# The 16 meta tokens' matmuls split over four column groups of TensorE

## What is computed

```python
def even_layer(x, ...):
    h = rms_norm(x, norm_g)
    proj = h @ w_in                               # 528 x 1024 @ 1024 x 3072
    q, k, v, gate_b, gate_c, u = jnp.split(proj, cuts, axis=-1)
    att = stick_breaking_attention(q, k, v)       # 8 heads of 64
    conv = gate_b * causal_short_conv(gate_c * u, conv_w)
    return jnp.concatenate([att, conv], axis=-1) @ w_out

def peer_ffn(x, ...):
    q = (hb @ w_query).reshape(t, 8, 2, 128)
    s = jnp.einsum('thpc,phkc->thpk', q, keys)
    sv, si = lax.top_k(s, 16)                     # then top 16 of the 16 x 16 sums
    u = expert_u[idx]
    act = gelu(einsum('tnd,td->tn', u, hb))
    return einsum('tn,tnd->td', gate * act, expert_v[idx])

for layer in range(2):
    h = h + even_layer(h) if layer == 0 else h + odd_layer(h)
    h = h + peer_ffn(h)
return h[:, 16:]
```

## Time and profile before

| | us |
|---|---|
| median of 3 runs | 3180.07 (3178.79 to 3183.22) |
| the profiled execution | 3176.12 |
| its span on the core | 3174.4 |
| PE busy | 2720.4 (86%) |
| DVE busy | 2100.6 (66%) |
| POOL busy | 997.9 (31%) |
| ACT busy | 596.8 (19%) |

### The profile page before, as it was taken

One profiled execution on the slowest core, in us unless ns is written; L12 is line 12 of the kernel. 1 busy time (PEld: TensorE's weight loads), 2 busy tenths in 40 slices (PEclk: granted clock), 3 DMA queues, 4 the chain that ended last, 5 costly groups with the idle time before them and its releaser, 6 DMA issues.

```text
span 3174.4 us, 29633 instructions
## 1 busy us (share of the span) xinstructions
PE 2720.4 (86%) x6788; PEld 1244.4 (39%) x6788; DVE 2100.6 (66%) x6388; ACT 596.8 (19%) x1775; POOL 997.9 (31%) x1106
## 2 busy tenths in 40 slices
PE   7999998898798879868898888878898898887777
PEld 3575343343343334324343333433344343333333
DVE  1123158888678767857688758875787678755554
ACT  1026211211111111112111221112112211111111
POOL 0000004333333333323333333333333333333332
PEclk9999999999999999989999999999999999889999
DMA  3121129999999999999999999999999999999998
GB/s 107 53 93 60 52 106 375 415 384 391 417 421 420 406 407 421 421 411 406 413 421 409 405 399 417 415 392 403 416 403 393 421 419 414 393 420 422 421 406 333
DMA packets 166368, 1135.00 MB, mean 358 GB/s; under 512 B 21136, under 2 KB 22160, under 8 KB 30768
## 3 DMA queue, kind: packets, MB, share of 16 engines
q0 software_dynamic: 149760, 1090.59, 84.0%
q1 hardware_dynamic: 16432, 42.62, 3.6%
HBM read 1130.97 MB, written 2.10 MB: 357 GB/s over the span
## 4 chain that ended last, share of the span: by engine, by line
DMA 43%; PE 39%; DVE 9%; issue 7%; ACT 1%; SPq 0%; POOLq 0%; DVEq 0%; ACTq 0%; POOL 0%
PE psum L1377 19%; DMA ring_early<-in_peer_uv,idx_u 12%; DMA ring_early<-in_peer_vu,idx_u 12%; DMA ring_late<-in_peer_uv,idx_u 10%; DMA ring_late<-in_peer_vu,idx_u 8%; PE psum L986 6%; PE psum L565 3%; PE psum L659 3%; DVE ring_early L1471 3%; PE psum L691 2%; PE psum L596 2%; DVE ring_late L1471 1%; DVE work L1112 1%; DVE si L1110 1%; PE psum L1018 1%
## 5 line engine op out<-in xcount | busy, mean ns | idle before, releaser
L1377 PE MATMUL psum<-ring_early,w_col 128*128 128x512 f32 x2864 | 1384.2, 627 | 234.2 <-ACT w_col L1424 203.7
L1471 DVE SCALAR_TENSOR_TENSOR ring_early<-ring_early,psum 128x1024 f32<-128x1024 f32 x716 | 871.2, 1217 | 440.8 <-DMA ring_early<-in_peer_vu,idx_u 225.7
L1377 PEld LDWEIGHTS psum<-ring_early,w_col 128*128 128x128 f32 x2864 | 565.7, 202 | 972.5 <-issue 732.7
L1377 PE MATMUL psum<-ring_late,w_col 128*128 128x512 f32 x1296 | 639.9, 633 | 124.0 <-ACT w_col L1424 94.1
L1358 POOL DMA_INDIRECT ring_early<-in_peer_vu,idx_u x360 | 339.2, 942 | 685.1 <-DVE ring_early L1471 300.5
L1358 POOL DMA_INDIRECT ring_early<-in_peer_uv,idx_u x356 | 337.2, 947 | 619.6 <-DVE ring_early L1471 302.0
L1471 DVE SCALAR_TENSOR_TENSOR ring_late<-ring_late,psum 128x1024 f32<-128x1024 f32 x324 | 394.6, 1218 | 204.6 <-DMA ring_late<-in_peer_uv,idx_u 133.6
L1424 ACT ACTIVATE w_col<-ident,weight 128x128 f32<-128x128 f32 x1024 | 343.4, 392 | 675.6 <-DVE weight L1453 660.0
L1377 PEld LDWEIGHTS psum<-ring_late,w_col 128*128 128x128 f32 x1296 | 256.6, 202 | 453.4 <-issue 325.4
L1418 ACT ACTIVATE ge<-ga 128x4 f32<-128x4 f32 x260 | 53.3, 205 | 1354.4 <-DVE ga L1439 1354.4
L986 PE MATMUL psum<-wq,hbT 128*128 128x512 f32 x512 | 276.7, 628 | 19.9 <-DVE work L1112 18.8
(11 more groups left out here) (220 smaller groups left out, 1785.1 us busy)
## 6 DMA issues: line engine op xcount, KB each, us to landing
wq<-in_peer_w_query SPq DMA_DIRECT2D x16, 1024.0 KB, 18.0
w_ring<-in_even_w_in SPq DMA_DIRECT2D x6, 2048.0 KB, 8.0
ring_early<-in_peer_vu,idx_u POOLq DMA_INDIRECT x360, 12.0
ring_early<-in_peer_uv,idx_u POOLq DMA_INDIRECT x356, 11.8
w_ring<-in_even_w_out SPq DMA_DIRECT2D x1, 4096.0 KB, 13.8
ring_late<-in_peer_vu,idx_u POOLq DMA_INDIRECT x162, 12.4
ring_late<-in_peer_uv,idx_u POOLq DMA_INDIRECT x162, 12.4
hres<-in_x SPq DMA_DIRECT2D x4, 512.0 KB, 4.9
```

What stands on the lines that cost most here:

```text
L1377: ins = nc.tensor.matmul(y_ps[:, half, :], w_col[:, i % W_SLOTS, :], v_cell(at)[:, 512 * half:512 * half + 512], start=False, stop=i == CH ...
L1471: nc.vector.scalar_tensor_tensor(out=cell, in0=cell, scalar=1.0, in1=rows, op0=ALU.mult, op1=ALU.mult, accum_out=dot[par][:, i:i + 1]).the ...
```

## The change

- Query, key and value of the meta tile: the 512 moving columns are cut in four of 128, each of which is multiplied into its own 32 partitions of the bank (partition 32c), for each k all four in turn. ACT brings them together with four copies of 16x128 instead of one of 16x512.
- The out-projection of the meta rows: 1024 columns in four of 256, in the same way, in one bank instead of two. PE adds the meta rows of `hres` through four identity matmuls, and ACT copies back with four copies of 16x256 where DVE added two halves. Projections are now counted from tile 0 (`i - 1`), and the waits on `s_proj` and `s_mix` are shifted by two to match.
- The meta queries: the four groups of `wq` go into four column groups, k outermost, with 32 stationary columns (16 tokens and 16 columns of zeros, cleared once by POOL). ACT then copies one 128x512 instead of four 16x512, PE transposes four 128x128 pieces instead of sixteen 16x128 ones, and ACT copies 128x512 again.
- The scores: still 16 matmuls of 128 columns, over the four column groups, into one bank.
- Top-k of the meta tokens reads that bank. The four spreading copies and the clearing of `cand` go. PE doesn't wait for them any longer before it transposes tile 0; before projection 4 it waits until top-k has read the bank (`s_read` 1).

```diff
@@ mixer_tensor
                     n = rows_of(t)
+                    if t == XT:
+                        for k in range(KD):
+                            for c in range(4):
+                                last = nc.tensor.matmul(psum[32 * c:32 * c + META, 4 + i % 4, 0:P], hT[:, k, cols_of(t)],
+                                                        w_ring[:, g % 2, k, P * c:P * c + P],
+                                                        start=(k == 0), stop=(k == KD - 1))
+                                if k == KD - 1 and c < 3:
+                                    last.then_inc(s_qkv_m, 1)
+                        last.then_inc(s_qkv_ps, 1)
+                        continue
...
             pe.wait_ge(s_qkv, 3 * TILES)
+            pe.wait_ge(s_qkv_mc, 9)
...
-            project_tensor(pe, 0)
-            project_tensor(pe, 1)
+            for c in range(4):
+                nc.tensor.matmul(psum[32 * c:32 * c + META, 0, 0:256], ident[0:META, 0:META], META_ROWS[:, 256 * c:256 * c + 256],
+                                 start=True, stop=False)
+            for k in range(KD):
+                for c in range(4):
+                    last = nc.tensor.matmul(psum[32 * c:32 * c + META, 0, 0:256], catT[:, k, cols_of(XT)],
+                                            w_out_sb[:, k, 256 * c:256 * c + 256], start=False, stop=(k == KD - 1))
+                    if k == KD - 1:
+                        last.then_inc(s_mproj, 1)
@@ project_tensor
-                pe.wait_ge(s_mix, max(i - 1, 4))
+                pe.wait_ge(s_mix, max(i - 3, 2))
+                pe.wait_ge(s_read, 1)
@@ mixer_scalar
+                    if t == XT:
+                        act.wait_ge(s_qkv_m, 3 * g + 3)
+                        for c in range(4):
+                            nc.scalar.copy(qkv[0:n, t, g, P * c:P * c + P], psum[32 * c:32 * c + META, 4 + i % 4, 0:P]
+                                           ).then_inc(s_qkv_mc if c < 3 else s_qkv, 1)
+                        continue
@@ start_tensor
-            if isinstance(job, int) and job == 1:
-                pe.wait_ge(s_spread, GROUPS)
-            elif isinstance(job, int) and job == 2:
+            if isinstance(job, int) and job == 2:
@@ meta_queries_tensor
-            for g in range(GROUPS):
-                for k in range(KD):
-                    last = nc.tensor.matmul(META_BANKS[g][0:META, :], hbT[:, k, 0:META], wq[:, k, 512 * g:512 * g + 512],
+            for k in range(KD):
+                for g in range(GROUPS):
+                    last = nc.tensor.matmul(FA[32 * g:32 * g + 32, :], hbT[:, k, 0:32], wq[:, k, 512 * g:512 * g + 512],
                                             start=(k == 0), stop=(k == KD - 1))
-                last.then_inc(s_meta_q_ps, 1)
-            for g in range(GROUPS):
-                pe.wait_ge(s_meta_q, g + 1)
-                for i in range(LISTS):
-                    at = META * (LISTS * g + i)
-                    last = nc.tensor.transpose(QUERY_BANK[:, at:at + META], META_Q[g][:, P * i:P * i + P], ident[0:META, 0:META])
+                    if k == KD - 1:
+                        last.then_inc(s_meta_q_ps, 1)
+            pe.wait_ge(s_meta_q, 1)
+            for i in range(LISTS):
+                last = nc.tensor.transpose(FB[:, P * i:P * i + P], q_sb[:, P * i:P * i + P], ident[:, :])
@@ meta_scores_tensor
-            for i in range(LISTS * GROUPS):
-                at = P * (i % LISTS)
-                last = nc.tensor.matmul(META_BANKS[i // LISTS][0:META, at:at + P], metaT[:, META * i:META * i + META],
-                                        keysT[:, i, :], start=True, stop=True)
+            for i in range(LISTS):
+                for g in range(GROUPS):
+                    last = nc.tensor.matmul(LATE_BANK[32 * g:32 * g + 32, P * i:P * i + P], q_T[:, i, 32 * g:32 * g + 32],
+                                            keysT[:, LISTS * g + i, :], start=True, stop=True)
+                    if i == LISTS - 1 and g < GROUPS - 1:
+                        last.then_inc(s_spread, 1)
@@ meta_scalar
-            for g in range(GROUPS):
-                act.wait_ge(s_meta_q_ps, g + 1)
-                nc.scalar.copy(META_Q[g], META_BANKS[g][0:META, :]).then_inc(s_meta_q, 1)
+            act.wait_ge(s_meta_q_ps, GROUPS)
+            nc.scalar.copy(q_sb[:, :], FA).then_inc(s_meta_q, 1)
             act.wait_ge(s_q_ps, 1)
-            nc.scalar.copy(metaT, QUERY_BANK[:, 0:LISTS * GROUPS * META]).then_inc(s_qT, 1)
-            act.wait_ge(s_cleared, 1)
-            act.wait_ge(s_sc, 1)
-            for g in range(GROUPS):
-                nc.scalar.copy(cand[32 * g:32 * g + META, :], META_BANKS[g][0:META, :]).then_inc(s_spread, 1)
+            nc.scalar.copy(q_T[:, :, :], FB.rearrange("p (a n) -> p a n", a=LISTS)).then_inc(s_qT, 1)
@@ topk_stages
-            lists = [(cand if meta else FA)[r, P * i:P * i + P] for i in range(LISTS)]
+            lists = [(LATE_BANK if meta else FA)[r, P * i:P * i + P] for i in range(LISTS)]
@@ scalar program
-            act.wait_ge(s_mix, 2)
+            act.wait_ge(s_mproj, 4)
+            for c in range(4):
+                nc.scalar.copy(META_ROWS[:, 256 * c:256 * c + 256], psum[32 * c:32 * c + META, 0, 0:256]).then_inc(s_mmix, 1)
+            act.wait_ge(s_mmix, 4)
@@ vector program
-            nc.vector.memset(cand[:, :], 0.0).then_inc(s_cleared, 1)
+            dve.wait_ge(s_mmix, 4)
```

More of the change, by code:

```diff
@@ L265, in program @@
         s_qkv = sem("qkv_copied")
+        s_qkv_m = sem("meta_qkv_multiplied")
+        s_qkv_mc = sem("meta_qkv_copied")
+        s_mproj = sem("meta_out_projected")
+        s_mmix = sem("meta_mixer_added")
         s_fm_ps = sem("conv_inputs_multiplied")
@@ L384, in mixer_sync @@
                         sp_.wait_ge(s_qkv_ps, TILES * (g - 1))
+                        sp_.wait_ge(s_qkv_m, 3 * (g - 1))
                     else:
@@ L432, in odd_weights_sync @@
         def odd_weights_sync(sp_):
-            sp_.wait_ge(s_proj, 2 * TILES)
+            sp_.wait_ge(s_proj, 2 * XT)
             sp_.dma_start(odd_g[:, :], odd_norm_g[0].rearrange("(k p) -> p k", p=P),
@@ L456, in mixer_constants @@
             c.did(nc.gpsimd.memset(conv_in[:, :, 0:2], 0.0))
+            c.did(nc.gpsimd.memset(hbT[:, :, META:2 * META], 0.0))
             c.settle()
@@ L471, in mixer_constants @@
             return c.n
-        MIXER_CONSTANTS = 20
+        MIXER_CONSTANTS = 21
         def expert_constants(pool):
@@ L503, in late_constants @@
         def late_constants(pool):
-            pool.wait_ge(s_proj, 2 * TILES)
+            pool.wait_ge(s_proj, 2 * XT)
             c = Steps(pool, s_late)
@@ L694, in add_projected @@
         def add_projected(dve, i):
-            dve.wait_ge(s_proj, i + 1)
+            dve.wait_ge(s_proj, i - 1)
             t, c = PROJECTED[i // 2], slice(512 * (i % 2), 512 * (i % 2) + 512)
@@ L701, in take_projected @@
         def take_projected(act, i):
-            act.wait_ge(s_proj, i + 1)
+            act.wait_ge(s_proj, i - 1)
             t, half = PROJECTED[i // 2], i % 2
@@ L828, in mixer_vector @@
                 dve.wait_ge(s_qkv, TILES + t + 1)
+                if t == XT:
+                    dve.wait_ge(s_qkv_mc, 6)
                 if t >= 2:
@@ L913, in mixer_vector @@
             softplus(HEADS - 1, 1)
-            add_projected(dve, 0)
-            add_projected(dve, 1)
         def norm_scalar(act, job, n, src):
@@ L1080, in program @@
         s_meta_q = sem("meta_queries_copied")
-        s_cleared = sem("meta_rows_cleared")
-        s_spread = sem("meta_rows_spread")
+        s_spread = sem("meta_scores_ready")
         s_routed_in = sem("key_numbers_as_floats")
@@ L1131, in lists_best @@
                 if meta:
-                    dve.wait_ge(s_spread, GROUPS)
-                else:
-                    dve.wait_ge(s_sc, piece + 1)
+                    dve.wait_ge(s_spread, GROUPS - 1)
+                dve.wait_ge(s_sc, piece + 1)
                 apart(dve)
@@ L1617, in _ @@
             keep_scalar(act, 0, None)
-            act.wait_ge(s_mix, 4)
+            act.wait_ge(s_mix, 2)
             norm_scalar(act, 1, P, tile_of(0))
@@ L1762, in _ @@
             project_tensor(pe, 6)
-            pe.wait_ge(s_mix, 6)
+            pe.wait_ge(s_mix, 4)
             first_query(1)
@@ L1776, in _ @@
             pe.wait_ge(s_setup, SETUP_STEPS)
-            pe.wait_ge(s_mix, 2 * TILES)
+            pe.wait_ge(s_mix, 2 * XT)
             open_sum(pe, None)
```

3 lines of the change are left out of this document (removed).

## The result

| | before | after |
|---|---|---|
| median, us | 3179.43 (3178.49 to 3183.22) | 3133.03 (3129.72 to 3135.28) |
| profiled execution, us | 3176.12 | 3131.68 |
| its span, us | 3174.4 | 3129.9 |
| PE busy, us | 2720.4 | 2674.6 |
| POOL may use the late ring groups at, us | 479.86 | 430.87 |

The ratio is 0.9851, with a 95% interval of 0.9837 to 0.9864: 46.4 us or 1.5% less, where 30.5 us were forecast. A second set of runs on another occasion gave 3133.69 and again 0.9851 (0.9836 to 0.9866).

A forecast was written before the change was run, and what follows sets the result against it. PE's list up to the last projection, then fixed-length gathers, was taken as the bound. 9.0 + 6.2 + 13.9 + 1.6 + 0.9 - 0.5 - 0.6 = 30.5 us saved gave 3149.6 us, range 3133 to 3168.

The forecast's parts named there:

- What bounds the kernel: PE's list until the last projection at 479.86 us, then gathers of fixed length; each microsecond saved before moves the end equally.
- Two streams at once: Meta-tile matmuls: at most two passes overlap, so each costs half its stream: 0.215 us at 512 columns, 0.107 at 256.
- my half: The assumed cost of a meta-tile pass, half of its stream; for the queries 13.8 us instead of 27.6.
- the first rival: All four column groups stream at once in the meta-tile matmuls: 40.5 us saved, 3139.6 us, chance 0.27.
- A floor of 0.063 us per pass: Least time per meta-tile pass, used for query, key, value (4.0 us per group g) and scores (2.0 us).
- The copies and waits around the matmuls: Beside the meta-tile matmuls: 0.5 us more for four copies, 0.6 more before the scores, 0.9 saved on spreading copies.
- The slow query: Tile 0's first query, 16 passes in 10.03 us instead of 7.03; expected to gain nothing unless it got faster.
- The cap of 2.3 us: Top-k, 15.5 us after the scores, limits the gain before tile 0's selection to some 2.3 us.
- Four at once: Rival: the second pass of a meta-tile matmul doesn't hold back the next column group; 40.5 us saved, 3139.6, chance 0.27.
- No overlap: Rival: the four column groups are streamed one after the other in the meta-tile matmuls; 3182 us, no change, chance 0.12.
- the emptying between groups: Rival: PE finishes before each column group change, 0.155 us for each of 360 passes, 56 us added; 3238, chance 0.08.
- The base: The whole kernel's time before, from which the saving was subtracted: the median 3180.1 us, 4.0 above the profiled execution.

The follow-up runs named there:

- Undoing one part: The changed kernel with the meta tile's query, key and value as before (512 columns, one column group, one copy): 3147.57 us, ratio 0.9901.
- sixteen in a row: The changed kernel with query, key, value pieces all in one column group and each group's 16 meta-query passes consecutive: 3164.15 us, ratio 0.9947.
- the first four experiments: Changed kernel with: one column group and sixteen passes consecutive, 3164.15 us; query, key, value undone, 3147.57; 64-column pieces, 3127.48; two column groups at a time, 3149.13.
- the later five: Changed kernel with eight passes consecutive, 3148.02 us; top-k reading a copy, 3135.92; unchanged again, 3133.69; attention product in two groups, 3127.87; exponential also split, 3120.38.

## Why the prediction was wrong

- **What bounds the kernel: right.** PE's list up to the last projection, then gathers of a fixed length. Undoing one part moved the end by 13.9 to 14.5 us, where the list said 14.5.
- **Two streams at once: wrong, and the largest error.** The step "The second must wait for the first. [...] Then at most two streams run at a time" took the timeline's order of starts for a rule about who blocks whom. The second pass of a matmul does wait for the first, but it waits at its column group, and up to three passes can do so before the others are held. With two or four passes in a row nothing is lost (7.08 and 7.14 us for the queries, where two streams would take 13.8). The program order, which spoke for my half, doesn't hold between column groups: with sixteen in a row, the next group's first pass starts after twelve. The step cost 10 us of the sum: this is the difference between 30.5 and the first rival's 40.5. The Trainium skill, "TensorEngine Tiling (Array Packing)", Theoretical Speedup, gives up to 4x for 32 columns; that was nearer than my reading of the rows: 27.64 us became 7.08, 3.9x.
- **A floor of 0.063 us per pass: wrong.** It was taken from the small transposes. Over four column groups, passes with 16 stationary columns start 0.016 us apart on average. Beyond the 40.5 us of the first rival it cost 6.0 us in query, key and value (14.5 - 8.5), 1.0 in the scores and 0.3 in the out-projection. Both errors went the same way, so the time fell out of the range by 0.3 us (3132.7 beside 3133). The range carried the error too, as its lower end allowed 0.04 and no less. What limits the transposes wasn't tested; their weight loads have 128 columns, where those here have 16 or 32.
- **The copies and waits around the matmuls: right within 0.2 us.** 1.31 us idle after the third group where 0.66 + 0.5 were expected, 0.97 us for the spreading copies where 0.9. PE comes to the scores 2.1 us behind the queries (2.17 expected). ACT's copies of the meta rows and their norm stayed under PE's tile 0.
- **The slow query.** "If its slow query gets faster, top-k (15.5 us after the scores) is next" came true where the query was faster: in the first profile it took 8.54 instead of 10.03 us, and 1.3 us were gained that the sum had at nothing. But that was the clock of one execution, not the change: in the second profile the query took 10.08 us and nothing was gained. The cap of 2.3 us held: with the 1.0 for the spreading copies the gain is 2.3 us in all, and in the run where the query had the full clock, PE waited for top-k instead.
- **The rivals.** Four at once was the right one, at 0.27; its time of 3139.6 was still too high by the floor. No overlap and the emptying between groups are refuted by every row.
- **The base.** I counted from the median of 3180.1, which was right: with a fourth run it was 3179.43, and the profiled execution lay 3.3 us below that.

## What to carry to other kernels

A matmul whose stationary side has few columns costs its full stream of moving columns; cut the moving side into as many pieces as there are free column groups and alternate between them at least every four passes (two float32 matmuls). A shortest duration found on one kind of instruction is no floor for another: bound it by zero as well. When a stage gets faster, look for the wait it had covered: in the attention the second half of the gain came only when the exponential behind it was split too.

## What the runs showed of the hardware

- Four column groups of 32 run four float32 streams side by side: 64 passes of 512 columns in 7.08 us, at 0.43 us per pass in each group. Two groups of 64 do so too: a head's product took 2.08 us instead of 3.36. Each column group takes about three waiting passes before it holds back the others (sixteen in a row 22.59 us, eight 15.85, four 7.14).
- 128 passes of 64 columns over four column groups, with a weight load each, take 1.98 us, 0.016 us apart on average.
- The granted clock fell to 0.50, the lower level of 1.2 GHz, in the out-projection of the meta rows in the first four experiments, but in none of the other six profiles with this change. What PE did before it doesn't tell the two apart: in the last 80 us its longest gap was 0.88 or 0.89 us in these four and 0.89 us in after, whose clock stayed at 1.00. The four were run together, on another chip than the later five; whether that or the moment made the difference stays open. It costs 1.7 us: 5.33 instead of 3.65 us for its 64 passes. Busy by stretch in the kernel with one column group for query, key and value, columns as in rows 2:

```profile
343.70:346.00 2.30, 2.23 (x36) 0.98 (x40) 0.09 (x1) 0.01 (x1) 1.78 (x9) 0.85 0.00 0
346.00:348.00 2.00, 2.00 (x24) 0.89 (x20) 0.00 (x0) 0.00 (x0) 1.14 (x7) 0.50 0.03 8
```

- The first query of tile 0, behind the run of small matmuls, ran partly at that level in ten of the eleven profiles (8.54 to 10.11 us for 16 passes; 7.03 at the full clock). The exception is the run with sixteen in a row: 7.13 us, and the clock fell only behind PE's 1.44 us of waiting for top-k (1.00 from 405 to 406 us, 0.50 from 407 to 410). So the step from tile 0's transposes to the selection took 14.11 us in one profile of after and 15.47 in the other. Single executions of that kernel differ by up to 5.6 us (3129.72 to 3135.28), and the rest wasn't traced.
